# Decay rows of the gated delta rule through DRAM, one exponential for both masks, and both moved three to four blocks earlier

## The chip, the cores and the metric

One core of a Trainium2 chip runs the kernel. The metric is the device time of one execution in microseconds (us). The engines are TensorE (PE, matrix products and transposes), VectorE (DVE), ScalarE (ACT), GpSimd (POOL) and SyncE (SP, which issues most of the weight loads). ACT and POOL issue DMAs too, each on a queue of its own.

## What is computed

The kernel is one layer of a decoder trunk for 512 prompt tokens and 8 x 8 sample tokens (576 in all, five tiles of at most 128). The change lies in the gated delta rule:

```python
g = -exp(a_log) * softplus(a + dt_bias)      # per token and head, 4 heads
G = cumsum(g)                                # inside the chunk (here: a tile)
diff = G[:, None] - G[None, :]               # G falls, so diff <= 0 where i >= j
dec = where(i >= j, exp(diff), 0)
a_mat = where(i > j, kk * dec * beta[:, None], 0)
qk = (q @ k.T) * dec
eG = exp(G)                                  # scales q, and k in the right-hand side
```

The kernel needs, for each tile and head, the mask `A` (i > j), the mask `D2` (the same values transposed: j >= i along the row), and `E`, which is exp(G) of all tokens of the tile on all 128 partitions.

## The kernel before

Every engine walks the same list of steps, `schedule()`, and does what a step asks of it (the `elif k0 == ...` branches of `build()`, one block of branches for each engine). So the list sets the order of the work on each engine and of the DMAs that the engine issues, and semaphores tie the engines together: `mm_wait` waits for a step's products, `ev_wait` for its evacuation from PSUM.

The change lies in the part with the 12 causal convolutions. For each channel block m from 2 to 11 the list holds `cv` m (PE: 16 products that fill a pair of PSUM banks, line 818; ACT copies them to SBUF, line 1506), `cvt` m (DVE: the convolution, lines 2040 to 2055), `cvs` m-1 (ACT: SiLU of the block before, line 1605), and then `between[m]`, other work that is spread over the blocks:

- block 4, `rN`: PE sums the squares of the retention's output (line 972), ACT takes the root (line 1608), `nr`: DVE the reciprocal (line 2064). Block 5, `ns`: ACT stores the rows in DRAM (`n_rows`, line 1614). Block 6, `nl`: ACT loads four of them, each broadcast to 128 partitions (line 1625, 4 x 288 KB). Blocks 7 and 8, `nf`: DVE scales with them (line 2069).
- block 7, `gC`: PE makes the cumulative sums by token on the partitions (lines 1022 and 1024), DVE copies them to `gcum`.
- blocks 7 and 8, `gG` t: PE makes the same sums along the row, on all 128 partitions, as four products whose weight is one column of `gl` broadcast to 128 (line 1015); ACT copies the bank to `Gr[t]`. `gD` t: DVE makes `Gr - gcum`, clipped at 0 from below into `A` and from above into `D2`, head by head (lines 2096 and 2097).
- blocks 9 and 10, `gE` t: ACT takes three exponentials of 512 columns and two of four columns (lines 1654 to 1658); POOL multiplies `A` and `D2` by their 0/1 masks (lines 2838 and 2840). `gX`: DVE takes the last column of each `E`.
- blocks 9 and 10, `gs` t: PE transposes k (line 1031), ACT squares it with a sum (line 1632). On PE a `gs` waits for SiLU of channel block 7: `pe.wait_ge(sem("conv"), 8)`.
- block 11, `gr`: the reciprocal and root of the sums. After it `rg` 0 and the products `gK` and `gQ` (line 1039).

Steps of the kinds in `PAIR` take the two pairs of PSUM banks in turn, those in `SINGLE` the four single banks in turn; `bank_free` makes PE wait until the step that had the bank before was evacuated. So block m's convolution waits for the evacuation of the step two pairs before, and `gs` 4 for that of `gs` 0. An evacuation counts in one semaphore for all of ACT's, and ACT works in the list's order.

SyncE loads the weights in chunks of 2 MB into a ring of three; the chunk `dz` is issued when the last product of convolution block 7 is done (`mm_wait(sp, plan.chunk_last[n - RING])`). ACT changes its function table between SiLU, the exponential and the root; `link` makes ACT wait for the end of an instruction of its own.

Of the kernel before, what the change touches and what calls it, by code (L numbers as in the profile page):

```python
# [19 lines left out]
F32 = mybir.dt.float32  # L20
# [5 lines left out]
P = 128  # L26
# [4 lines left out]
NT = 5  # L31
# [39 lines left out]
def ntok(t):  # L71
    return P if t < 4 else NB * LS
# [96 lines left out]
def schedule():  # L169

    s = [("tk", k) for k in range(6)] + [("ss",), ("tk", 6), ("xr",)] + [("tmq", t) for t in range(NT)]
    for t in range(NT):
# [3 lines left out]
        if t: s += [("rS", t - 1)]  # L176
# [4 lines left out]
    between = {2: [("nq", "rN", m) for m in (0, 1)], 3: [("nq", "rN", m) for m in (2, 3)],  # L181
               4: [("rN",), ("nr", "rN")], 5: [("ns", "rN")], 6: [("nl", "rN")],
               7: nf("rN", (0, 1)) + [("gC",), ("gG", 0), ("gG", 1), ("gD", 0), ("gD", 1)],
               8: nf("rN", (2, 3)) + [("gG", t) for t in range(2, NT)] + [("gD", t) for t in range(2, NT)],
               9: [("gs", t) for t in range(3)] + [("gE", 0), ("gE", 1)],
               10: [("gs", 3), ("gs", 4)] + [("gE", t) for t in range(2, NT)] + [("gX",)], 11: [("gr",)]}
    for m in range(2, NCONV):
# [89 lines left out]
def first_phase(e):  # L277
# [14 lines left out]

ACT_EVAC = {"ss", "tmq", "tmv", "rTk", "rO", "sO", "rO4", "rOt", "sO4", "sOt", "cv", "rN", "oN", "rg", "gG", "gs", "ab", "x2a", "x2b", "rt", "gA", "lY", "gW", "gU", "dz",
            "wx", "ux", "pp"}
DVE_EVAC = {"xr", "abT", "rTq", "rS", "rU", "rUs", "gC", "gK", "gQ", "lX", "lT", "gV", "gk", "sD", "sDs", "sU", "sUs", "wo", "wy", "uy",
            "rtT", "rank", "cnt", "x2c"}
# [70 lines left out]
def build(nc, a, o):  # L367
# [5 lines left out]
    u_rows = nc.dram_tensor("u_rows", (TOK, D), F32, kind="Internal").ap()  # L373
    n_rows = nc.dram_tensor("n_rows", (2 * P, TOK), F32, kind="Internal").ap()
    y_slots = nc.dram_tensor("y_slots", (SLOTS, D), F32, kind="Internal").ap()

    with ExitStack() as ctx:
        def sb(name, shape, dt=F32):
            return ctx.enter_context(nc.sbuf_tensor(name, shape, dt))
# [23 lines left out]
        beta = sb("beta", [P, NT, H])  # L403
        gcum = sb("gcum", [P, NT, 8])
        gx = sb("gx", [P, NT, 8])
        sm = sb("sm", [P, 3, NT, H])
# [264 lines left out]
        def heads(s, n, w):  # L671
            return single[plan.buf[s]][0:n, 0:H * w].rearrange("p (h w) -> p h w", h=H)

        def tri(t):
            return C("tri") if t < 4 else C("tri_s", 64)
# [14 lines left out]
        def mm_wait(eng, s):  # L690

            eng.wait_ge(s_mm, plan.mm[s])
# [107 lines left out]
        def _(pe):  # L800
# [24 lines left out]
            for s in STEPS:  # L825
# [184 lines left out]
                elif k0 == "gG":  # L1010
                    t, n = s[1], ntok(s[1])
                    pe.wait_ge(sem("g_beta"), 1)
                    out = heads(s, P, n)
                    for h in range(H):
                        last = nc.tensor.matmul(out[:, h, :], gl[0:n, t, h:h + 1].broadcast_to([n, P]), tri(t),
                                                start=True, stop=True)
                    last.then_inc(s_mm, 1)
# [475 lines left out]
        def _(act):  # L1493
# [13 lines left out]
            for s in STEPS:  # L1507
# [138 lines left out]
                elif k0 == "gG":  # L1646
                    t, n = s[1], ntok(s[1])
                    mm_wait(act, s)
                    act.wait_ge(sem("ret_free"), 1)
                    copy(Gr[t], heads(s, P, n)).then_inc(ev(k0), 1)  # L1650
                elif k0 == "gE":
                    t, n = s[1], ntok(s[1])
                    act.wait_ge(sem("gdiff"), t + 1)
                    nc.scalar.activation(A[t], A[t], ACT.Exp, scale=-1.0).then_inc(sem("gexp"), 1)
                    nc.scalar.activation(D2[t], D2[t], ACT.Exp).then_inc(sem("gexp"), 1)
                    nc.scalar.activation(E[t], Gr[t], ACT.Exp).then_inc(sem("gexp"), 1)
# [269 lines left out]
        def _(dve):  # L1926
# [22 lines left out]
            for s in STEPS:  # L1949
# [132 lines left out]
                elif k0 == "gC":  # L2082
# [7 lines left out]
                    V.tensor_tensor(sm[0:64, 2, 4, :], gcum[0:64, 4, 4:8], gcum[0:64, 4, 0:4], ALU.subtract)  # L2090
                elif k0 == "gD":
                    t, n = s[1], ntok(s[1])
                    ev_wait(dve, ("gG", t))
                    for h in range(H):

                        V.tensor_scalar(A[t][:, h, :], Gr[t][0:n, h, :], gcum[0:n, t, h:h + 1], 0.0, ALU.subtract, ALU.max)
                        last = V.tensor_scalar(D2[t][:, h, :], Gr[t][0:n, h, :], gcum[0:n, t, h:h + 1], 0.0, ALU.subtract, ALU.min)
                    last.then_inc(sem("gdiff"), 1)
                elif k0 == "gX":
                    dve.wait_ge(sem("gexp"), 5 * NT)  # L2100
                    for t in range(NT):
# [666 lines left out]
        def _(pool):  # L2768
# [3 lines left out]
            for s in STEPS:  # L2772
# [59 lines left out]
                elif k0 == "gE":  # L2832
                    t, n = s[1], ntok(s[1])
                    if t == 0:
                        pool.wait_ge(sem("nfin"), 4)
                        G.memset(nwz, 0.0).then_inc(sem("zeroed"), 1)
                    pool.wait_ge(sem("gexp"), 5 * t + 1)
                    G.tensor_tensor(A[t], A[t], bh(C("low") if t < 4 else C("low_s", 64), n, n), ALU.mult).then_inc(sem("gmask"), 1)
                    pool.wait_ge(sem("gexp"), 5 * t + 2)
                    G.tensor_tensor(D2[t], D2[t], bh(tri(t), n, n), ALU.mult).then_inc(sem("gmask"), 1)  # L2840
# [200 lines left out]
```

## Time and profile before

| | us |
|---|---|
| median of 3 runs | 823.36 (823.05 to 825.56) |
| the profiled execution, its own time | 822.85 |
| its span, first to last instruction | 821.0 |
| PE busy | 802.8 (98%) |
| DVE busy | 405.6 (49%) |
| ACT busy | 214.8 (26%) |
| POOL busy | 152.6 (19%) |

The profile is one execution. The time of an execution holds some 2 us outside the span. In the rows a product of 32-bit floats counts as two records of PE (a transpose as one), L818 is line 818 of the kernel, and times are from the start of the span. "Idle before" names what released the engine. The engines PE and ACT start an instruction before the last one has left the pipeline, so starts tell more than durations.

### The profile page before, as it was taken

What the parts mean: (1) busy time and instruction counts of PE and PEld (TensorE: products, weight loads), DVE (VectorE), ACT (ScalarE), POOL (GpSimd) and SP (SyncE); (2) the same over time, 40 slices, a digit from 0 to 9 for tenths busy, and PEclk for the clock granted to TensorE, in tenths of its full rate; (3) what the DMA queues carried; (4) which work ended last, traced back from release to release, by engine and by line L of the source; (5) the groups of instructions that cost most, each with busy time, mean ns of one, the idle gap of its engine ahead of it and who ended that gap; (6) DMA issues with size and microseconds to landing.
All of it is one profiled execution on the core that took longest, in us unless ns stands there. A gap on an engine that the chain in (4) does not pass through costs nothing. (4 is left out here: it accounts for less than half of the span.)

```text
span 821.0 us, 12877 instructions
## 1 busy us (share of the span) xinstructions
PE 802.8 (98%) x5172; PEld 504.8 (61%) x5172; DVE 405.6 (49%) x886; ACT 214.8 (26%) x469; POOL 152.6 (19%) x182
## 2 busy tenths in 40 slices
PE   9999999999999999999999999999999999999995
PEld 4446777887889987777777776455433333334443
DVE  4223556684666522663853458826352101104976
ACT  3202152239324311131101110122121111125275
POOL 0324420004055223300220034000100001004100
PEclk9999999999999999999999999999999999999999
DMA  9521344503020200514241123134899999995211
GB/s 360 229 85 32 120 166 154 157 18 111 1 104 3 77 29 14 204 52 124 103 177 65 67 103 119 65 131 183 308 397 362 421 426 423 402 400 204 77 52 65
DMA packets 20977, 135.23 MB, mean 165 GB/s; under 512 B 2437, under 2 KB 3077, under 8 KB 13749
## 3 DMA queue, kind: packets, MB, share of 16 engines
q1 hardware_dynamic: 13328, 103.08, 32.1%
q0 software_dynamic: 4720, 23.83, 7.9%
q10 hardware_dynamic: 2868, 7.47, 3.0%
q8 instruction: 43, 0.70, 0.3%
q14 instruction: 18, 0.14, 0.0%
HBM read 118.94 MB, written 19.63 MB: 169 GB/s over the span
## 5 line engine op out<-in xcount | busy, mean ns | idle before, releaser
L818 PE MATMUL pair<-mem 128*128 128x288 f32 x640 | 158.9, 408 | 0.0
L818 PEld LDWEIGHTS pair<-mem 128*128 128x128 f32 x640 | 120.3, 190 | 35.6 <-ACT mem L1506 2.1
L986 PE MATMUL single<-mem 128*128 128x288 f32 x448 | 110.0, 407 | 0.2
L986 PEld LDWEIGHTS single<-mem 128*128 128x128 f32 x448 | 84.7, 190 | 25.7 <-issue 1.6
L1373 PE MATMUL single<-mem 128*32 128x512 f32 x768 | 85.1, 594 | 0.9 <-DVE mem L2539 0.9
L1506 ACT ACTIVATE mem<-pair 128x512 f32<-128x512 f32 (+5 forms) x83 | 36.5, 487 | 162.6 <-PE pair L818 63.1
L1506 ACT ACTIVATE mem<-single 128x256 f32<-128x256 f32 (+5 forms) x109 | 44.6, 419 | 126.9 <-PE single L1234 48.5
L2532 DVE SCALAR_TENSOR_TENSOR mem<-single,mem 128x256 f32<-128x256 f32 x12 | 5.8, 484 | 102.3 <-PE single L1373 91.4
L1373 PEld LDWEIGHTS single<-mem 128*32 128x32 f32 x768 | 23.6, 110 | 52.8 <-issue 51.7
L1225 PE MATMUL pair<-mem 128*128 128x512 f32 x112 | 51.0, 601 | 0.0
L1442 PE MATMUL pair<-mem 128*128 128x512 f32 x112 | 49.4, 595 | 0.3 <-DVE mem L2600 0.3
L2251 DVE TENSOR_TENSOR mem<-mem,single 128x288 f32<-128x288 f32 x40 | 18.1, 453 | 55.7 <-PE single L986 52.2
L1321 PE MATMUL pair<-mem 128*32 128x512 f32 x384 | 43.9, 595 | 0.0
L1442 PEld LDWEIGHTS pair<-mem 128*128 128x128 f32 x112 | 20.7, 190 | 25.2 <-issue 24.4
L1225 PEld LDWEIGHTS pair<-mem 128*128 128x128 f32 x112 | 20.3, 190 | 21.7 <-issue 21.4
L881 PE MATMUL pair<-mem 128*128 128x512 f32 (+1 forms) x96 | 32.1, 525 | 0.0
L2938 POOL DMA_INDIRECT mem<-u_rows,ids x12 | 11.4, 947 | 110.6 <-PE single L1306 100.8
L1007 PE MATMUL pair<-mem 128*128 128x288 f32 x112 | 28.4, 409 | 0.3 <-DVE mem L2303 0.2
L857 PE MATMUL pair<-mem 128*128 128x512 f32 x64 | 28.2, 595 | 0.4 <-DVE mem L1960 0.4
L2049 DVE SCALAR_TENSOR_TENSOR mem<-mem,vec 128x512 f32<-128x512 f32 x36 | 27.9, 774 | 1.3
L1007 PE MATMUL single<-mem 128*128 128x288 f32 x112 | 27.8, 406 | 0.0
L1007 PEld LDWEIGHTS pair<-mem 128*128 128x128 f32 x112 | 21.0, 190 | 7.0 <-DVE mem L2303 1.5
(431 smaller groups left out, 1118.1 us busy)
## 6 DMA issues: line engine op xcount, KB each, us to landing
mem<-in_w_gu SPq DMA_DIRECT2D x17, 2048.0 KB, 14.4
mem<-in_w_down SPq DMA_DIRECT2D x17, 1024.0 KB, 13.2
y_slots<-mem SPq DMA_DIRECT2D x9, 512.0 KB, 10.5
y_slots<-in_zeros POOLq DMA_DIRECT2D x8, 512.0 KB, 8.6
mem<-in_w_ga SPq DMA_DIRECT2D x2, 2048.0 KB, 7.7
mem<-in_w_gb SPq DMA_DIRECT2D x2, 2048.0 KB, 7.6
mem<-in_w_wo SPq DMA_DIRECT2D x2, 2048.0 KB, 7.7
mem<-in_w_pg SPq DMA_DIRECT2D x2, 2048.0 KB, 16.6
```

The lines of the kernel that those rows point to most:

```text
L818: last = nc.tensor.matmul(pb[:, hf, 0:HALF], w(k), rhs[:, k, hf * HALF:(hf + 1) * HALF], start=(k == 0), stop=(k == kk - 1))
L857: last = nc.tensor.matmul(q_bank[t][rows, cols], uT[:, k, t * P:t * P + ntok(t)], ring[0][:, 512 * k + cols.start:512 * k + cols.stop], st ...
L881: last = nc.tensor.matmul(pair[plan.buf[s]][rows, 0, cols], uT[:, k, t * P:t * P + ntok(t)], w[:, k, cols], start=(k == 0), stop=(k == KD ...
L986: last = nc.tensor.matmul(single[plan.buf[s]][:, 0:HALF], lhs[:, k, :], rhs[:, k, :], start=(k == 0 and j in (0, 1, 3, 4)), stop=(k == 3), ...
L1007: last = nc.tensor.matmul(fast_bank(s), lhs[:, k, :], rhs[:, k, :], start=(k == 0 and j in (0, 1, 3, 4)), stop=(k == 1), skip_group_check= ...
L1225: last = nc.tensor.matmul(sx_bank[j], rows[:, u, v, :], wgt[:, u, 512 * v:512 * v + 512], start=(i == 0 and j < 5), stop=(i == 3), skip_gr ...
L1321: last = nc.tensor.matmul(pair[p % 2][BS * g:BS * g + BS, n, :], hT[p % 2][:, k, BS * g:BS * g + BS], w_dn[e % 4][:, k, n * 512:(n + 1) * ...
L1373: last = nc.tensor.matmul(single[3][BS * g:BS * g + BS, :], xT[p % 2][:, k, BS * g:BS * g + BS], w_gu[e % 4][:, k, :], start=(k == 0), sto ...
L1442: last = nc.tensor.matmul(bank, rows(c), weights(c), start=(start and c == 0), stop=(c == 3), skip_group_check=True)
L1506: copy = lambda out, in_, scale=1.0: nc.scalar.activation(out, in_, ACT.Copy, scale=scale)
L2049: V.scalar_tensor_tensor(out=acc[m % 2][:, 0:LP], in0=cbuf[m % 2][:, j:j + LP], scalar=conv_w[:, m, j:j + 1], in1=acc[m % 2][:, 0:LP], op0 ...
L2251: V.tensor_tensor(to, plus, single[plan.buf[s]][:, 0:HALF], ALU.add).then_inc(ev(k0), 1)
```

## The change

`gC` and `gG` move to block 4, ahead of `rN`. `gG` is now one step: two products whose weights are `gl` itself (16 and 4 columns), so that the sums of all tiles and heads come out as rows on 20 partitions. DVE copies them to a new tile `grow`, ACT stores that in DRAM (`g_rows`, two DMAs), and in block 6 the new step `gL` loads five tiles of `Gr` from it, each broadcast to 128 partitions (4 x 256 KB, and 128 KB for tile 4, whose rows have 64 columns). `gD` goes. `gE` moves to blocks 7 and 8: ACT makes |Gr - gcum| with four `Abs` for each tile, then one exponential of its negative for both masks, and `E`; it waits until all five loads have landed. POOL writes `A` from `D2`, then masks `D2` in place. `gX` moves from block 10 to block 8. `gs` stays where it is, and k's squares are still made from transposes.

```diff
@@ schedule
-               4: [("rN",), ("nr", "rN")], 5: [("ns", "rN")], 6: [("nl", "rN")],
-               7: nf("rN", (0, 1)) + [("gC",), ("gG", 0), ("gG", 1), ("gD", 0), ("gD", 1)],
-               8: nf("rN", (2, 3)) + [("gG", t) for t in range(2, NT)] + [("gD", t) for t in range(2, NT)],
-               9: [("gs", t) for t in range(3)] + [("gE", 0), ("gE", 1)],
-               10: [("gs", 3), ("gs", 4)] + [("gE", t) for t in range(2, NT)] + [("gX",)], 11: [("gr",)]}
+               4: [("gC",), ("gG",), ("rN",), ("nr", "rN")], 5: [("ns", "rN")], 6: [("nl", "rN"), ("gL",)],
+               7: nf("rN", (0, 1)) + [("gE", 0), ("gE", 1)], 8: nf("rN", (2, 3)) + [("gE", t) for t in range(2, NT)] + [("gX",)],
+               9: [("gs", t) for t in range(3)], 10: [("gs", 3), ("gs", 4)], 11: [("gr",)]}
@@ TensorE, gG
-                    t, n = s[1], ntok(s[1])
                     pe.wait_ge(sem("g_beta"), 1)
-                    out = heads(s, P, n)
-                    for h in range(H):
-                        last = nc.tensor.matmul(out[:, h, :], gl[0:n, t, h:h + 1].broadcast_to([n, P]), tri(t),
-                                                start=True, stop=True)
+                    out = single[plan.buf[s]]
+                    nc.tensor.matmul(out[0:16, 0:P], gl[:, 0:4, :], tri(0), start=True, stop=True)
+                    last = nc.tensor.matmul(out[32:32 + H, 0:64], gl[0:64, 4, :], tri(4), start=True, stop=True)
                     last.then_inc(s_mm, 1)
@@ ScalarE, gG, gL and gE
-                    t, n = s[1], ntok(s[1])
-                    mm_wait(act, s)
+                    ev_wait(act, s)
+                    act.dma_start(g_rows[0:16, :], grow[0:16, :]).then_inc(sem("g_stored"), 16)
+                    act.dma_start(g_rows[16:20, 0:64], grow[32:36, 0:64]).then_inc(sem("g_stored"), 16)
+                elif k0 == "gL":
+                    act.wait_ge(sem("g_stored"), 32)
                     act.wait_ge(sem("ret_free"), 1)
-                    copy(Gr[t], heads(s, P, n)).then_inc(ev(k0), 1)
+                    for t in range(NT):
+                        n = ntok(t)
+                        act.dma_start(Gr[t], g_rows[4 * t:4 * t + 4, 0:n].unsqueeze(0).broadcast_to([P, H, n])).then_inc(sem("g_rows"), 16)
                 elif k0 == "gE":
                     t, n = s[1], ntok(s[1])
-                    act.wait_ge(sem("gdiff"), t + 1)
-                    nc.scalar.activation(A[t], A[t], ACT.Exp, scale=-1.0).then_inc(sem("gexp"), 1)
-                    nc.scalar.activation(D2[t], D2[t], ACT.Exp).then_inc(sem("gexp"), 1)
+                    ev_wait(act, ("gC",))
+                    act.wait_ge(sem("g_rows"), 16 * NT)
+                    for h in range(H):
+                        last = nc.scalar.activation(D2[t][:, h, :], Gr[t][0:n, h, :], ACT.Abs, bias=gcum[0:n, t, h:h + 1], scale=-1.0)
+                    link(last)
+                    nc.scalar.activation(D2[t], D2[t], ACT.Exp, scale=-1.0).then_inc(sem("gexp"), 1)
                     nc.scalar.activation(E[t], Gr[t], ACT.Exp).then_inc(sem("gexp"), 1)
@@ VectorE, gD goes, gG comes
-                elif k0 == "gD":
-                    t, n = s[1], ntok(s[1])
-                    ev_wait(dve, ("gG", t))
-                    for h in range(H):
-
-                        V.tensor_scalar(A[t][:, h, :], Gr[t][0:n, h, :], gcum[0:n, t, h:h + 1], 0.0, ALU.subtract, ALU.max)
-                        last = V.tensor_scalar(D2[t][:, h, :], Gr[t][0:n, h, :], gcum[0:n, t, h:h + 1], 0.0, ALU.subtract, ALU.min)
-                    last.then_inc(sem("gdiff"), 1)
+                elif k0 == "gG":
+                    mm_wait(dve, s)
+                    V.tensor_copy(grow[0:16, :], single[plan.buf[s]][0:16, 0:P])
+                    V.tensor_copy(grow[32:36, 0:64], single[plan.buf[s]][32:36, 0:64]).then_inc(ev(k0), 1)
@@ GpSimd, gE
-                    pool.wait_ge(sem("gexp"), 5 * t + 1)
-                    G.tensor_tensor(A[t], A[t], bh(C("low") if t < 4 else C("low_s", 64), n, n), ALU.mult).then_inc(sem("gmask"), 1)
-                    pool.wait_ge(sem("gexp"), 5 * t + 2)
+                    pool.wait_ge(sem("gexp"), 4 * t + 1)
+                    G.tensor_tensor(A[t], D2[t], bh(C("low") if t < 4 else C("low_s", 64), n, n), ALU.mult).then_inc(sem("gmask"), 1)
+                    pool.wait_ge(sem("gmask"), 2 * t + 1)
                     G.tensor_tensor(D2[t], D2[t], bh(tri(t), n, n), ALU.mult).then_inc(sem("gmask"), 1)
```

## Rows read from the trace of the kernel before

**Rows 1.** The page: span, and busy time by engine.
```profile
span 821.0 us, 12877 instructions
...
PE 802.8 (98%) x5172; PEld 504.8 (61%) x5172; DVE 405.6 (49%) x886; ACT 214.8 (26%) x469; POOL 152.6 (19%) x182
```

**Rows 2.** Windows: length, busy us by engine, PE clock, DMA share, GB/s.
```profile
85.00:205.00 120.00, 120.00 (x660) 92.17 (x659) 74.53 (x211) 52.38 (x140) 25.77 (x31) 1.00 0.34 114
```

**Rows 3.** PE in order of time: start, us, operation, count of records.
```profile
134.78 23.55 PE L818 MATMUL pair<-mem 128*128 128x288 f32 x96
158.17 0.52 PE L1022 MATMUL single<-gl,const 128*128 128x16 f32 x4
...
158.93 2.05 PE L1015 MATMUL single<-const,gl 128*128 128x128 f32 x16
160.82 7.93 PE L818 MATMUL pair<-mem 128*128 128x288 f32 x32
168.58 2.98 PE L1015 MATMUL single<-const,gl 128*128 128x128 f32 x24
171.49 8.03 PE L818 MATMUL pair<-mem 128*128 128x288 f32 x32
179.36 1.47 PE L1031 MATMUL single<-const,mem 128*128 128x128 f32 x12
...
188.43 1.04 PE L1031 MATMUL single<-const,mem 128*128 128x128 f32 x8
```

**Rows 4.** ACT's order of time, the last issues of `nl`.
```profile
151.52 0.94 ACTq L1625 DMA_DIRECT2D mem<-n_rows  x2
```

**Rows 5.** DVE's order of time, the reciprocal of block 4.
```profile
138.27 3.75 DVE L2064 RECIPROCAL mem<-mem 128x576 f32<-128x576 f32 x1
```

**Rows 6.** Line 1625, window 150 to 160: its DMAs.
```profile
L1625 ACTq DMA_DIRECT2D mem<-n_rows x4: 333/454/456, 150.7 to 152.0; - x4
...
DMA to landing us min/median/max: 3.7/5.7/6.8
```

**Rows 7.** Windows with `n_rows` loading, and with `dz` loading.
```profile
156.00:158.00 2.00, 2.00 (x10) 1.58 (x9) 0.00 (x0) 0.00 (x0) 0.00 (x0) 1.00 0.79 167
...
162.00:164.00 2.00, 2.00 (x10) 1.54 (x9) 2.00 (x4) 0.00 (x0) 0.00 (x0) 1.00 0.99 426
```

**Rows 8.** SyncE's order of time, the issue of `dz`.
```profile
158.36 0.33 SPq L715 DMA_DIRECT2D mem<-in_w_dz  x1
```

**Rows 9.** DMAs: SyncE's queue (q1), and ACT's third load.
```profile
q1 hardware_dynamic: 13328, 103.08, 32.1%
...
w_rt<-in_w_rt ACTq DMA_DIRECT2D x1, 128.0 KB, 4.8
```

**Rows 10.** ACT's order of time at the start of the kernel.
```profile
1.66 0.45 ACTq L1496 DMA_DIRECT2D w_rt<-in_w_rt  x1
...
6.26 0.68 ACT L1512 ACTIVATE mem<-mem 128x576 f32<-128x576 f32 x1 [1.35 <-DMA mem<-in_xT]
```

**Rows 11.** ACT's order of time in blocks 9 and 10.
```profile
184.01 1.28 ACT L1654 ACT_TABLE_LOAD   x1
185.31 0.63 ACT L1654 ACTIVATE mem<-mem 128x512 f32<-128x512 f32 x1
185.84 0.61 ACT L1655 ACTIVATE mem<-mem 128x512 f32<-128x512 f32 x1
...
187.07 0.61 ACT L1654 ACTIVATE mem<-mem 128x512 f32<-128x512 f32 x1
...
191.46 0.26 ACT L1632 ACTIVATE mem<-single 128x128 f32<-128x128 f32 x1
191.62 0.19 ACT L1632 ACTIVATION_READ_ACCUMULATOR mem<-single 128x1 f32 x1
```

**Rows 12.** ACT's order of time, copies with and without a pointer.
```profile
62.60 0.69 ACT L1569 ACTIVATE mem<-pair,rcol 128x512 f32<-128x512 f32 x1 [8.73 <-PE single L956]
63.19 0.59 ACT L1506 ACTIVATE mem<-pair 128x512 f32<-128x512 f32 x1
```

More of the change, by code:

```diff
@@ L290 @@
             "wo": lambda s: 13 + s[2]}
-ACT_EVAC = {"ss", "tmq", "tmv", "rTk", "rO", "sO", "rO4", "rOt", "sO4", "sOt", "cv", "rN", "oN", "rg", "gG", "gs", "ab", "x2a", "x2b", "rt", "gA", "lY", "gW", "gU", "dz",
+ACT_EVAC = {"ss", "tmq", "tmv", "rTk", "rO", "sO", "rO4", "rOt", "sO4", "sOt", "cv", "rN", "oN", "rg", "gs", "ab", "x2a", "x2b", "rt", "gA", "lY", "gW", "gU", "dz",
             "wx", "ux", "pp"}
-DVE_EVAC = {"xr", "abT", "rTq", "rS", "rU", "rUs", "gC", "gK", "gQ", "lX", "lT", "gV", "gk", "sD", "sDs", "sU", "sUs", "wo", "wy", "uy",
+DVE_EVAC = {"xr", "abT", "rTq", "rS", "rU", "rUs", "gC", "gG", "gK", "gQ", "lX", "lT", "gV", "gk", "sD", "sDs", "sU", "sUs", "wo", "wy", "uy",
             "rtT", "rank", "cnt", "x2c"}
@@ L374, in build @@
     n_rows = nc.dram_tensor("n_rows", (2 * P, TOK), F32, kind="Internal").ap()
+    g_rows = nc.dram_tensor("g_rows", (NT * H, P), F32, kind="Internal").ap()
     y_slots = nc.dram_tensor("y_slots", (SLOTS, D), F32, kind="Internal").ap()
@@ L404, in build @@
         gcum = sb("gcum", [P, NT, 8])
+        grow = sb("grow", [P, P])
         gx = sb("gx", [P, NT, 8])
@@ L2090, in _ @@
                     V.tensor_tensor(sm[0:64, 2, 4, :], gcum[0:64, 4, 4:8], gcum[0:64, 4, 0:4], ALU.subtract)
-                elif k0 == "gD":
-                    t, n = s[1], ntok(s[1])
-                    ev_wait(dve, ("gG", t))
-                    for h in range(H):
-                        V.tensor_scalar(A[t][:, h, :], Gr[t][0:n, h, :], gcum[0:n, t, h:h + 1], 0.0, ALU.subtract, ALU.max)
-                        last = V.tensor_scalar(D2[t][:, h, :], Gr[t][0:n, h, :], gcum[0:n, t, h:h + 1], 0.0, ALU.subtract, ALU.min)
-                    last.then_inc(sem("gdiff"), 1)
+                elif k0 == "gG":
+                    mm_wait(dve, s)
+                    V.tensor_copy(grow[0:16, :], single[plan.buf[s]][0:16, 0:P])
+                    V.tensor_copy(grow[32:36, 0:64], single[plan.buf[s]][32:36, 0:64]).then_inc(ev(k0), 1)
                 elif k0 == "gX":
-                    dve.wait_ge(sem("gexp"), 5 * NT)
+                    dve.wait_ge(sem("gexp"), 4 * NT)
                     for t in range(NT):
```

## Prediction

> **What bounds the kernel now.** I read the page first: TensorE (PE) is busy for 98% of the span, VectorE (DVE) for half of it, ScalarE (ACT) for a quarter [rows 1]. The reader is to see that only PE's time, or a wait of PE, can move the end. The busy times by stage say the same of the place of the change: between 85 and 205 us PE is busy for all of the 120 us, at full granted clock [rows 2]. So an instruction removed from PE there shortens the kernel by its whole cost, and other work costs nothing until it makes PE wait. PE's own order of time gives the beat [rows 3]: the 96 records of convolution blocks 5 to 7 (32 a block) take 23.4 us, 7.8 a block. Lastly I read ACT's order of time and its DMAs, since the change hands ACT the new work [rows 4 to 12].
>
> **What goes from PE.** The 20 products `gG` (40 records, 16 and 24) fill 158.93 to 160.82 and 168.58 to 171.49, thus 1.89 + 2.91 = 4.80 us [rows 3]. Two products take their place in block 4: one of 128 columns, one of 64, with few weight columns. A `gG` product took 0.24 us; `gC`'s first two took 0.52 with far fewer columns [rows 3]. Between 0.2 and 0.5, I take 0.4. `gC` moves and costs the same. PE gains 4.4 us in all; the bounds are 4.3 and 4.6.
>
> **DVE and POOL.** `gD`'s 40 instructions go, from cover (no PE wait is there), so they bring nothing. The masks on POOL stay ten instructions; the second of each tile now waits for the first, and they are done before `gK` is evacuated, tens of us later. They may meet DVE's convolution of block 9; each convolution has a block of cover. Nothing.
>
> **Block 4.** ACT now waits there for `gG`'s evacuation before it does `rN`'s root, and the root, the table load and all of ACT behind it wait too. DVE does it after convolution 4, so from 138.27, where the reciprocal `nr` began [rows 5]: some 0.9 us of small copies, two DMA issues at 0.47 [rows 4], a table load of 1.28 and the root of 0.74 put the root's end near 142.1. PE needs that bank at block 6, at 134.78 + 1.2 + 7.8 = 143.8 (the 1.2 is what `gC` and `gG` add to block 4). It is covered by 1.7 us. `nr` then ends near 145.8, and its row is stored 2 us later, before the loads of block 6. Nothing, if the issues stay under 1.2 us each.
>
> **The five loads of `gL`: when the rows are there.** They stand on ACT's queue behind the four loads of `n_rows`. These were issued until 152.5 and landed 3.7 to 6.8 us after issue [rows 4, 6], as if one after another, so the last near 158.6; the block now starts 1.2 later, so 159.8. The DMA windows show that the 4 x 288 KB moved at some 170 GB/s with the engines 79% busy [rows 7], which makes 6.7 us of them, and by the landings, from 152 on, 6.2: a broadcast of rows is slow. `gL` is 4 x 256 KB of the same kind (1024/1152 of 6.2: 5.5) and a fifth of 128 KB, whose rows of 64 columns are 512 pieces of 256 B. By bytes it is 0.7 us, by pieces (n_rows had as many) 6.2; I take 2. Alone they would be there at 159.8 + 5.5 + 2 = 167.3 (166.0 to 171.5).
>
> They are not alone. SyncE issues the 2 MB of `dz` when block 7 ends on PE, at 158.4 before [rows 8] and 159.5 now. At 426 GB/s [rows 7] that is 4.9 us of all engines. At the start of the kernel, where both queues are full, the third DMA of ACT's queue landed at 1.66 + 4.8 = 6.5 us, and ACT's second piece of xT, the third DMA of SyncE's, at 6.26 [rows 9, 10]: the queues advance turn by turn. SyncE's packets are large (7.7 KB) and few, `gL`'s small and many [rows 9], so all of `dz` gets in before `gL` ends. That makes 172.2; without any delay 167.3. I take 171, and 166 to 173 as the bounds.
>
> The Trainium skill ("DMA: Bandwidth & Descriptors", Queues, rings and completion order) says that each engine goes round between the queues packet by packet, draining a whole packet of several descriptors; by it `dz` is in front of the last of `gL` too, and the sum would be that of 172. The trace agrees in the start's two landings, as far as they go.
>
> **ACT from there.** `gE` of tile 0 waits for all five rows; behind it on ACT stand `gE` 1, the evacuation of block 8, `silu` 7, `gE` 2 to 4, the evacuation of block 9, `silu` 8 and `gs` 0. PE waits for two of them: `gs` 0 on PE needs `silu` 7, and `gs` 4 on PE takes the bank that ACT frees with `gs` 0 (the fourth single bank before it). Costs:
> - A tile's three exponentials and two small ones took 187.07 - 185.31 = 1.76 [rows 11]; its exponentials start 0.53 apart, so one less leaves 1.24. Four `Abs` of 128 columns with a pointer bias are not in the trace. The nearest are the 128-column instructions of `gs`, 0.27 long, the next operation 0.16 later [rows 11], and 512 columns with a pointer scale, 0.69 against about 0.60 without [rows 12]. So 0.16 to 0.29 apart, and the link waits out the last. I take 1.2 for four (0.7 to 1.3): 2.45 a tile. Tile 4 (half the columns): about 1.8. Five tiles: 11.6.
> - Two loads of the exponential table and two back, 1.28 each [rows 11]: 5.1. Two `silu`: 1.3. Two evacuations: 1.5. `gs` 0: 1.0, and 0.1 of signals.
> Sum 20.6 us from the landing (18.5 to 21.5). The Trainium skill ("ScalarE: Activation LUTs", What ACT_TABLE_LOAD costs) adds 1.38 us of drain to each load; here the exponential starts 1.30 after the load began [rows 11], so the trace disagrees. By the page the chain would be 5.5 longer.
>
> **The sum.** PE wants `gs` 4 at 188.43 + 0.44 - 4.4 = 184.5 [rows 3]. Landing 171 + 20.6 = 191.6, so PE waits 7.1 us: about 5.0 at `gs` 0 (171 + 9.0 for `gE` 0, 1, table loads, evacuation and `silu` 7 = 180.0, against 179.36 - 4.4 = 175.0), the rest at `gs` 4. What stands later (block 11's evacuation, the key norms, `gK`) has a block's cover again. Net: -4.4 + 7.1 = **+2.7 us**. The profiled execution took 822.85 (span 821.0 and 1.85 around it), so 825.6 for it; its time is 0.5 under the median of 823.36, so the median comes to **826.1**. Break-even is a landing at 168.3; the full gain needs 163.9.
>
> **Rivals.**
> 1. The rows are there at about 167, because `dz` and the broadcasts overlap (the engines are not full during `n_rows`). Wait 3.1, net -1.3: 822.1. Against: the two landings at the start.
> 2. (Other side.) ACT's chain has the cover. The mechanism is one: the rows land by 163.9 on ACT's queue (the broadcast of short rows runs at the rate of `dz`, 1.15 MB in 2.7 us, from 159.8 or earlier). Then nothing waits, 4.4 is gained: 819.0. For: PE had not one wait from 85 to 205, and ACT was busy 52 of those 120 us [rows 2]. Against: `n_rows` at half that rate. It is faster than the measurement can tell up to a landing of 165.8.
> 3. `Abs` needs a table that has no exponential. Then each tile loads twice: 2.57 x 5 = 12.8 more, 839. Against: copies and squares run between `silu`s with no load. The Trainium skill ("ScalarE: Activation LUTs", Table sets) lists abs in every set, which the runs will show.
> 4. The fifth load costs its 6.2 us by pieces, or a wait of 5 us on PE brings more behind it (a lower granted clock, which no row here shows after such a wait). Net +7: 830.
>
> **How the numbers follow.** The chance of the forecast is 0.50 (its own range 824 to 829: landing 169 to 172.5, chain 20 to 21.5), of rival 1 0.20, rival 2 0.18, rival 3 0.02, rival 4 0.10. What a measurement can tell from no change is 0.3%, 2.5 us: faster is under 820.9, slower over 825.8. Rival 2 and a little of rival 1 make faster: 0.20. Most of rival 1 and the forecast with a landing below 170.7 make the same: 0.32. The rest, 0.48, is slower. The range takes in a landing of 168 with the shortest `Abs` (net -2.4) up to one of 173 with the long chain (+5.6): 820.9 to 829.0.
>
> **What would show it.** In the changed profile: PE's blocks 5 to 8 in one piece and about 1.2 us late; block 9 right behind block 8, 3.2 early in total; DMAs of `g_rows` landing 15 us or more after issue, the last near 171; an ACT wait of about 10 us before the first `Abs`, released by that DMA; PE idle some 5 us before `gs` 0 and 2 before `gs` 4, released by ACT; no PE wait at blocks 5 and 6; `gK` starting 2.7 later than 204.82. The prediction is wrong if the rows land before 166, if `Abs` runs in 0.16 us, or if PE's `gs` has no wait.

## The result, and the profile after

The changed kernel took **826.96 us** (median of 11 runs, 823.96 to 831.54), the kernel before beside it 823.24 (11 runs, 822.82 to 825.94): ratio 1.0040, 95% interval 1.0021 to 1.0059. It is slower by 3.7 us, against a forecast of 826.1. Note the range: 7.6 us for the changed kernel, 3.1 for the other. The changed kernel was measured a second time, beside later experiments: 825.43, ratio 1.0021.

The page of the changed kernel, to be read against [rows 1]: PE works 2.3 us less, yet the span is 4.1 longer.

```profile
span 825.1 us, 12781 instructions
...
PE 800.5 (97%) x5136; PEld 501.5 (61%) x5136; DVE 400.7 (49%) x848; ACT 216.1 (26%) x479; POOL 152.8 (19%) x182
```

PE in order of time, over the stretch of [rows 3]:

```profile
134.45 0.39 PE L1013 MATMUL single<-const,gl 128*16 128x128 f32 x2
134.78 0.27 PE L1014 MATMUL single<-const,gl 64*4 64x64 f32 x2
134.98 1.18 PE L972 MATMUL pair<-mem,const 128*32 128x288 f32 x16
136.09 39.07 PE L818 MATMUL pair<-mem 128*128 128x288 f32 x160
179.21 2.08 PE L1029 MATMUL single<-const,mem 128*128 128x128 f32 x12 [4.06 <-ACT mem L1603]
181.09 9.06 PE L818 MATMUL pair<-mem 128*128 128x288 f32 x32
189.99 0.60 PE L1029 MATMUL single<-const,mem 128*128 128x128 f32 x4
191.05 0.63 PE L1029 MATMUL single<-const,mem 128*64 128x128 f32 x4 [0.46 <-ACT mem L1630]
191.51 15.69 PE L818 MATMUL pair<-mem 128*128 128x288 f32 x64
207.03 5.19 PE L1037 MATMUL single<-mem 128*128 128x128 f32 x45
```

The two products that replace the 20 take 0.53 us (134.45 to 134.98). Blocks 5 to 9 now run in one piece of 160 records. Then PE waits 4.06 us in front of `gs` 0, for silu 7 (SiLU of channel block 7, L1603). Block 10, 7.93 us long before, takes 9.06. The windows say why (window, its length, PE's busy time and records, granted clock, DMA share, GB/s):

```profile
178.00:180.00 2.00, 0.79 (x7) 0.99 0.00 0
180.00:182.00 2.00, 2.00 (x9) 0.50 0.00 0
182.00:184.00 2.00, 2.00 (x7) 0.65 0.00 0
184.00:186.00 2.00, 2.00 (x10) 1.00 0.00 0
```

After the wait PE ran for some 3.4 us at the lower of its two levels (1.2 GHz); before the wait it had been busy without a gap. The last four records of `gs` wait 0.46 more. `gK` starts at 207.03, 2.21 later than before.

ACT in order of time, from the issue of the loads to the first masks:

```profile
153.87 5.73 ACTq L1655 DMA_DIRECT2D mem<-g_rows  x5
159.78 0.41 ACT L1504 ACTIVATE mem<-pair 128x288 f32<-128x288 f32 x1 [6.52 <-PE pair L818]
...
169.95 1.28 ACT L1661 ACTIVATE mem<-mem,gcum 128x128 f32<-128x128 f32 x4 [8.83 <-DMA mem<-g_rows]
171.24 1.28 ACT L1663 ACT_TABLE_LOAD   x1
172.54 0.63 ACT L1663 ACTIVATE mem<-mem 128x512 f32<-128x512 f32 x1
...
173.78 1.26 ACT L1661 ACTIVATE mem<-mem,gcum 128x128 f32<-128x128 f32 x4
175.07 0.63 ACT L1663 ACTIVATE mem<-mem 128x512 f32<-128x512 f32 x1
...
178.38 0.68 ACT L1603 ACTIVATE mem<-mem 128x576 f32<-128x576 f32 x1
...
189.28 0.68 ACT L1603 ACTIVATE mem<-mem 128x576 f32<-128x576 f32 x1
189.87 0.26 ACT L1630 ACTIVATE mem<-single 128x128 f32<-128x128 f32 x1
```

ACT stood for 8.83 us until the rows were there, at 169.9. From then on it has no gap up to `gs` 0, which frees the bank that PE takes at 191.05. Line 1655, the five loads:

```profile
L1655 ACTq DMA_DIRECT2D mem<-g_rows x5: 387/1269/1527, 153.9 to 158.5; - x5
...
DMA to landing us min/median/max: 7.4/8.3/11.3
```

### The profile page after: what moved, and what is told of

Read it like the earlier page. It is cut to its first block and busy times, and to the rows that moved or that the text cites. A ratio compares the mean times of both kernels' runs of the same rounds, so it can differ in the third digit from the quotient of the medians.

```text
span 825.1 us, 12781 instructions
## 1 busy us (share of the span) xinstructions
PE 800.5 (97%) x5136; PEld 501.5 (61%) x5136; DVE 400.7 (49%) x848; ACT 216.1 (26%) x479; POOL 152.8 (19%) x182
## 5 line engine op out<-in xcount | busy, mean ns | idle before, releaser
L818 PE MATMUL pair<-mem 128*128 128x288 f32 x640 | 159.6, 410 | 0.0
L1504 ACT ACTIVATE mem<-single 128x256 f32<-128x256 f32 (+6 forms) x104 | 41.9, 413 | 126.9 <-PE single L1232 48.5
L1319 PE MATMUL pair<-mem 128*32 128x512 f32 x384 | 43.9, 595 | 0.0
```

Source lines behind the costliest of these rows:

```text
L818: last = nc.tensor.matmul(pb[:, hf, 0:HALF], w(k), rhs[:, k, hf * HALF:(hf + 1) * HALF], start=(k == 0), stop=(k == kk - 1))
L1319: last = nc.tensor.matmul(pair[p % 2][BS * g:BS * g + BS, n, :], hT[p % 2][:, k, BS * g:BS * g + BS], w_dn[e % 4][:, k, n * 512:(n + 1) * ...
L1504: copy = lambda out, in_, scale=1.0: nc.scalar.activation(out, in_, ACT.Copy, scale=scale)
```

## The experiments

The reading to be tested: the loss is the landing of the rows plus ACT's chain behind it, all else is covered. The first four runs take the change apart. Each time is the median, with the lowest and highest in brackets, and each ratio is to the kernel before measured beside it.

**Rows a block earlier.** In block 6's list the copies stand; here in block 5's:

```
-  5: [("ns", "rN")], 6: [("nl", "rN"), ("gL",)],
+  5: [("ns", "rN"), ("gL",)], 6: [("nl", "rN")],
```

> The changed kernel with the copies of the decay rows (gL: stores by ACT, loads back by ACT's queue) in block 5 instead of block 6, three blocks ahead of the exponentials; nothing else differs. Theory (the chain behind the landing is on the path only because the rows land at 169.9): the rows land near 155 to 160, the first decay mask is made 10 us sooner, PE never waits for ACT in front of gs, its clock stays at 1.00 there, and the time is about 819 us, 0.5% under the kernel before. Rival A (the ACT work of block 7 itself, table loads and the pointer biases, is too long for the slot wherever the rows are): ACT is late again, a wait of 2 us or more in front of the gs products stays, and the time is 823 or more. Rival B (stores and loads in block 5 delay the column norms' scratch round trip or the evacuation of convolution 6): a new wait of PE near 100 to 140, time 821 or more.

Measured: 820.22 (819.63 to 822.07, 7 runs; before 823.16), ratio 0.9963 (0.9950 to 0.9976). The five issues took 2.34 us in place of 5.73, the loads landed 3.9 to 4.9 us after issue, ACT began the first `Abs` at 160.97 behind silu 6 without a wait, and PE ran through:

```profile
175.07 1.47 PE L1029 MATMUL single<-const,mem 128*128 128x128 f32 x12
176.38 7.93 PE L818 MATMUL pair<-mem 128*128 128x288 f32 x32
184.14 1.04 PE L1029 MATMUL single<-const,mem 128*128 128x128 f32 x8
185.01 15.69 PE L818 MATMUL pair<-mem 128*128 128x288 f32 x64
200.54 8.38 PE L1037 MATMUL single<-mem 128*128 128x128 f32 x80
```

`gK` starts 4.28 earlier than before: that is the saving on PE in full, so the landing's theory holds and both rivals fall. But the end came only 3.2 earlier (span 817.8), not 4.3, and the time is 1.2 above the 819 expected. The missing 1.1 is the subject of the last group.

**`dz` later.** SyncE issues `dz` only when PE has done convolution 9, so that it no longer moves beside the rows.

```
+                if name == "dz":
+                    mm_wait(sp, ("cv", 9))
```

> The changed kernel with one more wait: SP loads dz only when PE has done convolution 9, so that the big load is no longer beside the rows' load back. Theory (some of the landing time is the shared engines): the rows land 3 to 4 us sooner, near 166, PE waits under 1 us and its clock does not drop, time about 821 to 822 us. Rival (the rows' load takes what it takes, because of its small pieces and broadcast reads): landing stays at 169 to 170, time 826 to 827. If dz itself comes too late, a wait near its first use shows it.

Measured: 822.77 (821.35 to 823.73, 10 runs), ratio 0.9983 (0.9973 to 0.9994); profiled run: rows at 165.7, PE waits 1.3 us at `gs` 4 and nowhere else, clock at 1.00. The range shrank to 2.4 us. So `dz` beside the loads costs 4.2 us of median against the first measurement of the changed kernel, 2.7 against the second. PE's wait was a little over the 1 us expected.

**Exponentials where they were.** `gE` and `gX` in blocks 9 and 10, copies of the rows in block 6.

> The changed kernel with the exponentials and masks (gE, gX) back in blocks 9 and 10, where the kernel before has them; the copies of the rows stay in block 6. Theory (the loss comes from ACT waiting in block 7 on rows that are not there, with silu 7 queued behind): no such wait, PE runs through, the gain of the products left out comes out in full, 819 us. Rival (the move is harmless and the form costs: Abs, pointer bias, DMA beside the convolutions): a wait moves to block 9 or later and the time is 823 to 827.

Measured: 824.54 (822.96 to 826.40, 12 runs), ratio 1.0011 (1.0001 to 1.0020). There was no wait at `gs`, but one at `gK`, as the rival had it.

**The single exponential alone.** The kernel before without `gD`: ACT makes the four `Abs` and one exponential of each tile in blocks 9 and 10. ScalarE's part of the edit (DVE's `gD` goes, and POOL reads `D2`, as in the change):

```
-                    act.wait_ge(sem("gdiff"), t + 1)
-                    nc.scalar.activation(A[t], A[t], ACT.Exp, scale=-1.0).then_inc(sem("gexp"), 1)
-                    nc.scalar.activation(D2[t], D2[t], ACT.Exp).then_inc(sem("gexp"), 1)
+                    ev_wait(act, ("gC",))
+                    ev_wait(act, ("gG", t))
+                    for h in range(H):
+                        last = nc.scalar.activation(D2[t][:, h, :], Gr[t][0:n, h, :], ACT.Abs, bias=gcum[0:n, t, h:h + 1], scale=-1.0)
+                    link(last)
+                    nc.scalar.activation(D2[t], D2[t], ACT.Exp, scale=-1.0).then_inc(sem("gexp"), 1)
```

> The kernel before with one part alone: one exponential of minus the absolute difference serves both masks; the rows are still made by products on PE and the work stays in its old blocks. Theory (ACT is off the path there): no change, 823.3 us, within 0.3%. Rival (Abs sits in another table set than Exp): ten more table loads in the trace and 823 to 830 us.

Measured: **827.88** (825.32 to 828.99, 6 runs), ratio 1.0047 (1.0032 to 1.0061). The table-set rival fell too: no load stands between `Abs` and the exponential of a second tile. So the theories of both runs fell, in the same place. PE of the single exponential alone, in order of time:

```profile
206.76 3.73 PE L1039 MATMUL single<-mem 128*128 128x128 f32 x32
212.77 6.54 PE L1039 MATMUL single<-mem 128*128 128x128 f32 x48 [2.27 <-DVE mem L2120]
```

and DVE in the same stretch:

```profile
205.31 0.32 DVE L2099 COPY glast<-mem 128x4 f32<-128x4 f32 x1 [7.75 <-ACT gx L1661]
...
207.77 0.75 DVE L2052 SCALAR_TENSOR_TENSOR mem<-mem,vec 128x512 f32<-128x512 f32 x1
...
211.59 1.13 DVE L2120 SCALAR_TENSOR_TENSOR mem<-single,kr,mem 128x128 f32<-128x128 f32 x4
```

A tile now takes ACT 2.54 us in place of 1.76 [rows 11], for four short instructions cost more than one long one saves. Over five tiles that is 3.7 us: DVE's `gX`, which waits 7.75 us for ACT, begins at 205.31 against 199.65, of which 1.94 are this execution's later start. The taps of a convolution stand behind `gX` on DVE, and behind them the first evacuation of `gK`, for which PE waits 2.27 us. Then it runs at half clock again. With the exponentials back in blocks 9 and 10, where the wait is the same 2.27, the windows (PE alone, in the order given above) show

```profile
204.00:206.00 2.00, 0.28 (x3) 1.00 0.00 0
206.00:208.00 2.00, 1.45 (x7) 0.57 0.00 0
208.00:210.00 2.00, 2.00 (x12) 0.57 0.00 0
```

2.27 of wait and 1.75 of half clock are 4.0 us: from `gK`'s start to the next block it is 12.34 us (200.55 to 212.89), 8.32 before. So ACT's work in blocks 9 and 10 was not free. In the kernel before, DVE's first evacuation of `gK` ended near 207.4 and PE wanted the bank 3.73 after its start, at 208.55: it was 1.2 us ahead.

**Smaller pieces.** Tile 4's rows in a tensor of their own (`g_tail`), so that its load has 128 pieces of 1 KB in place of 512 of 256 B.

> The changed kernel with tile 4's rows in a contiguous tensor of their own, so that its load back has 128 pieces of 1 KB in place of 512 of 256 B; block 6 as before. Theory of the prediction (tile 4's small pieces cost 2 us of the landing, 0.7 to 6.2): the first load lands 1 to 2 us sooner than 169.9, the wait of PE in front of gs 0 falls from 4.1 to 2 or 3 us, time 824 to 825.5. Rival (the five loads share one 5 us stretch with dz, and bytes set it): landing within 0.5 us of 169.9, time 826.5 to 827.5.

Measured: 823.55 (821.11 to 826.89, 10 runs), ratio 1.0009 (0.9990 to 1.0027).

**Busy wait.** Spare products on PE in front of `gs` 0:

```
+                    if t == 0:
+                        for i in range(14):
+                            nc.tensor.matmul(single[plan.buf[s]][:, 0:P], C("ones"), C("tri"), start=True, stop=True)
```

> The changed kernel with 14 spare products of 128 columns (about 3.4 us) written to gs 0's bank before PE waits for silu 7; they are overwritten and change no result. PE is thus busy for most of the 4.1 us that it waits in the changed kernel. Theory (the wait also costs the clock, 1.7 us after it): the granted clock stays at 1.00 from 180 to 184 and the time is 825 us or a little more, 1.2 to 1.9 under the changed kernel's in the same job. Rival (the clock falls anyway or its loss is not 1.7): 826.5 to 828.

Measured: 825.00 (821.52 to 829.82, 10 runs), ratio 1.0031 (1.0008 to 1.0053).

These two are inconclusive, and taught something else. In the profiled run with spare products the loads were the changed kernel's to the letter, but ACT began at 164.97, so there was no wait that the products could have filled. The median lies 2 us under the first measurement of the changed kernel and 0.4 under the second, below. What the clock costs was thus not measured, but the first profile of the changed kernel argues that a full clock would have brought nothing there. PE reaches the last four records of `gs` at 190.59 and waits until 191.05, when ACT's chain gives the bank. Had block 10 run at full clock, PE would have waited there for as much longer. By this reading my price of 1.7 us for the clock was wrong: half clock took the place of waiting.

**Both in block 5, and 72 waits.** First the tail's tensor with the copies in block 5.

> The copies of the rows in block 5 and tile 4's rows in a tensor of their own, both. Theory (in block 5 the landing has some 5 us to spare, so small pieces cost nothing there): equal to the version with block 5 alone, 820.2 us within 0.5, and PE waits nowhere for ACT in front of gs. Rival (small pieces disturb other transfers too): 0.5 us or more under it.

Measured: 820.34 (819.60 to 820.90, 6 runs), ratio 0.9965 (0.9953 to 0.9978), as its theory had it: in block 5 the small pieces cost nothing. Then the same with waits in PE's stream, in front of the products of each step k of convolutions 2 to 10:

```
+                    if s[0] == "cv" and 2 <= s[1] <= 10:
+                        pe.wait_ge(sem("rtmp_ones"), 1)
```

> The same as the kernel with block 5 and the tail's own tensor, with 72 waits on a semaphore that has long been there added to PE's stream, one in front of each k step of convolutions 2 to 10: they cost PE nothing while its products run, and put PE's later instructions 72 places further on, about where they stand in the kernel before. In the changed kernel and in the three variants without the 20 products, PE stands for 1.43 us at one and the same product of L1060, near 245, with nothing that the trace shows it waiting for; in the kernel before and in the one that keeps the products, it does not. Theory (this pause depends on the place of the instructions in PE's stream): it is gone or at another place, and the time is about 1.4 us under the kernel without the waits, near 818.8. Rival (it comes from other engines or from DMA at that time): the pause of 1.43 stays at that product and the time is the same, 820.2.

Measured: 820.75 (819.49 to 821.64, 10 runs), ratio 0.9971 (0.9962 to 0.9981). It said nothing on its question: its page counts 12781 instructions, as without the waits, so they made PE's stream no longer. It is a second measurement of the kernel above.

**The changed kernel again, and a semaphore for each load.** The first has no edit. In the second, where the wait for all five loads stood before tile 0, each tile waits for its own (the loads' side of the edit is left out here):

```
-                    act.wait_ge(sem("g_rows"), 16 * NT)
+                    act.wait_ge(sem(("g_rows", "ld_vec", "ld_const", "ld_small", "ld_head")[t]), (16, 32, 32, 64, 32)[t])
```

Each load adds 16 to a semaphore of its own; four of them served loads of the kernel's start and stand at a known count.

> The changed kernel once more, nothing altered, beside the two others. In the profiled runs so far the last of the five loads of the rows landed at 169.9 (changed kernel), and near 165 in the two variants with the same copies in block 6 and dz at the same time. Theory (the last load lands either ahead of dz's transfer or behind it, by chance of the execution, and that is where the changed kernel's wide range of times comes from): median 825 to 828, range over 4 us; if this profiled run lands at 165, it has a span of 820 to 822 and no wait in front of gs 0. Rival (those variants landed early for what they change): landing at 169.5 to 170.5 again, span 824 to 826.

> The changed kernel with a semaphore of its own for each of the five loads of the rows, so that tile 0's absolute differences wait for tile 0's rows alone and not for all five; copies in block 6, dz and all else as in the changed kernel. Theory (only the last load is late; the first lands near 161.5, and ACT's work of 2.5 us a tile keeps behind the landings): ACT starts tile 0 near 161.5, PE waits nowhere in front of gs, span 817.5 to 819, time 820.0 to 820.8, and the range is as narrow as in the kernel with the copies in block 5. Rival (the loads land together, or a later tile's load holds ACT up): ACT waits 2 us or more in a later tile, time 822 to 827.

Measured: the changed kernel again 825.43 (822.45 to 827.68, 10 runs), ratio 1.0021 (1.0006 to 1.0035). Its profiled run, in PE's order of time:

```profile
177.76 1.50 PE L1029 MATMUL single<-const,mem 128*128 128x128 f32 x12
179.10 7.93 PE L818 MATMUL pair<-mem 128*128 128x288 f32 x32
186.86 0.60 PE L1029 MATMUL single<-const,mem 128*128 128x128 f32 x4
189.60 0.63 PE L1029 MATMUL single<-const,mem 128*64 128x128 f32 x4 [2.14 <-ACT mem L1630]
```

No wait at `gs` 0, full clock, 2.14 us at `gs` 4. (The span, 823.6, misses the 820 to 822 expected since this execution had lost 2.5 us by block 4, in its first 30 us; such losses of up to 2.5 us came in executions of several kernels, such as 1.9 in the one with the single exponential alone; their cause was not looked for.) ACT began the masks 31.0 us after PE began `rN` (168.49 against 137.47), in the first profile 35.0 (169.95 against 134.98), and in the runs with the tail's tensor, the spare products and `dz` later 30.8, 29.9 and 29.8. The longest landing was 8.4 us in these, 11.3 in the first, and 11.9 with the exponentials in blocks 9 and 10. The DMA view of the stretch of the issues, first profile and then second, tells which load it is:

```profile
mem<-g_rows ACTq DMA_DIRECT2D x4, 256.0 KB, 8.2
mem<-g_rows ACTq DMA_DIRECT2D x1, 128.0 KB, 11.3
...
mem<-g_rows ACTq DMA_DIRECT2D x4, 256.0 KB, 8.0
mem<-g_rows ACTq DMA_DIRECT2D x1, 128.0 KB, 7.5
```

The load of tile 4 alone is late. Over the seven profiled runs with the copies in block 6 the other four have a median of 7.9 to 8.6 us from issue to landing; tile 4's takes 11.3 and 11.9 in two of them and 6.4 to 7.5 in five (7.1 of these with its pieces of 1 KB, 6.4 without `dz`). So with `dz` beside the loads, tile 4's comes some 4 to 5 us later in some executions than in others. That, and the losses of the first 30 us, are what the profiles show of the changed kernel's wide range; the highest time, 831.54, is 2 us more than the two together give (826.89 and 2.5), and was not profiled.

With a semaphore for each load: **820.57** (819.72 to 822.30, 7 runs), ratio 0.9968 (0.9956 to 0.9980), as its theory said. ACT starts tile 0 at 163.26, and PE has no wait at `gs`, although the loads landed as late as 9.1 us after issue (tile 4's, in this execution, 6.9):

```profile
163.26 1.28 ACT L1662 ACTIVATE mem<-mem,gcum 128x128 f32<-128x128 f32 x4 [1.71 <-DMA mem<-g_rows]
```

Thus not the rows as such were late: tile 0 waited for tile 4's. That the range is as narrow as with the copies in block 5 suggests that a late load of tile 4 no longer matters; no profile caught one.

**The rows alone.** Last, the other half of the change: sums in block 4 and DRAM copies in block 5, the differences on DVE, the two exponentials and the scaling in their old blocks.

> The kernel before with the rows alone changed: sums of 16 and 4 rows made in block 4, stored and loaded back through DRAM in block 5; the differences on DVE (blocks 7 and 8), the two exponentials and the scaling (blocks 9 and 10) as in the kernel before. Theory (the products left out give 4.2 us, a pause of 1.4 us comes at L1060, and the single exponential with its 20 small absolute differences is what cost 4.7 us where it was tried alone in the old place): 820 to 821 us, 2 to 3 under the kernel before. PE now comes 4.3 us sooner to gK, whose first bank DVE had free 1.25 us before PE wanted it; if ACT's work of blocks 9 and 10 does not move forward with PE, PE waits there for DVE, up to 3 us, and the clock may fall after it: 821 to 825. Rival (the cost of the single exponential in the old place came from the earlier PE or from the place, not from the form): a wait of 2.3 us at gK and half clock here too, 824 to 825.

Measured: 820.33 (819.88 to 824.01, 5 runs), ratio 0.9965 (0.9951 to 0.9979). No wait at `gK`: PE's 80 records took 8.38 us. ACT's and DVE's work there moved forward with PE (DVE's first evacuation ended near 204.9, and PE wanted the bank at 206.0). The whole gain is in the rows; the single exponential adds none, and costs 4.7 us in blocks 9 and 10.

**The pause at L1060.** In all ten profiled runs that leave the products out and add nothing to PE's stream, PE stood for 1.2 to 1.7 us before one and the same record, the 175th of the inverse's leaves (64 columns each), with nothing that the trace shows it waiting for. Here in the kernel with the copies in block 5:

```profile
239.72 1.10 PE L1060 MATMUL single<-mem 64*64 64x64 f32 x29
242.25 1.65 PE L1060 MATMUL single<-mem 64*64 64x64 f32 x41 [1.43 <-issue]
```

To move the place of PE's later instructions, 18 spare products of one column were put in front of `gs` 0 in that kernel:

> The kernel with the copies in block 5, and 18 spare products of one column in front of gs 0 (written to its bank and overwritten), which put back about as many instructions in PE's stream as the products left out had (72 of the 72 that the page counts fewer on PE). The 72 added waits of the run before were not in the program that ran: its page counts 12781 instructions, as without them, so that run said nothing. In the run with 14 spare products (55 instructions more on its page) the pause of L1060 came 27 records earlier. Theory (the pause is tied to a place in PE's instruction stream, and falls on short products of L1060 only because 18 products are gone): no pause of over 0.5 us at L1060, and the time is 820.2 plus what the 36 short records cost (1 to 2.5 us) less 1.4, so 820 to 821.5. Rival (the pause belongs to the work of that moment): 1.2 to 1.4 us at the same product, time 821 to 822.7.

Measured: 828.36 (827.25 to 829.63, 4 runs), ratio 1.0068 (1.0053 to 1.0082), far outside what I expected: 36 records of one column took 4.37 us, 0.12 each (the 1 to 2.5 us expected are 0.03 to 0.07), and from 180.8, while they still ran, the clock was at half for 3.4 us, though PE's records show no gap. But its 71 more instructions moved the pause 35 records forward, out of L1060's products:

```profile
245.11 2.21 PE L1084 MATMUL single<-mem 64*64 64x64 f32 x66
248.94 0.39 PE L1084 MATMUL single<-mem 64*64 64x64 f32 x4 [1.62 <-issue]
```

In the run with 14 spare products, 55 more instructions moved it 27 records forward. A record is two instructions (weights and product), so 70 and 54: the pause sits at a fixed place in PE's stream of instructions. The theory that PE has no such pause at all once its stream is as long as in the kernel before fell. What is loaded at such a place can be seen in the DMA view of single stretches: the queue named instruction moves packets of 16 KB. With the copies in block 5, from 240 to 242:

```profile
q1 hardware_dynamic: 46, 0.57, 68.6%
q8 instruction: 1, 0.02, 3.0%
```

The next such packet comes from 242 to 244, then one from 246 to 248. The 2 MB of `in_w_ga` (q1, issued at 234.82) move just ahead of and beside the first of them, and fill the engines from 238 to 240. In the kernel before such a packet came from 236 to 238, before that load (issued at 239.10), and the next from 244 to 246. I take it that PE's next instructions were late because their packet was behind the weights' packets: argued from the trace, not tried (the way would be to move `in_w_ga`).

## Why the prediction was right

By its steps:

- **PE's saving**: forecast 4.4, measured 4.28 (`gK` in the kernel with the copies in block 5); the two new products took 0.53, not 0.4.
- **DVE and POOL, nothing**: right for this schedule, with the exponentials in blocks 7 and 8. That it was nothing is owed to the move: in blocks 9 and 10 ACT's extra 0.78 us a tile came through DVE to PE as 4 us. I had looked for PE's waits there and found none, but not for how far DVE was ahead.
- **Block 4**: the root ended at 142.44 (forecast 142.1), PE had its bank in time. The proviso, issues under 1.2 us each, held for the two stores (0.35 and 0.57). The sum had no term for the issues of the five loads of block 6, 1.27 us the median one. They held ACT until 159.6, and it evacuated convolution 7 at 159.78, just in time. So the loads landed 7.4 to 11.3 after issue, not 15 or more; the rest of the delay was in the issuing.
- **Landing**: forecast 171 (166 to 173), 169.9 in this profile, about 4 to 5 us sooner in others: two outcomes, and the forecast value was the late one. That the profile of the result was a late one is luck. `dz` is the cause that I gave, and taking it away brought 2.7 to 4.2 us. Without it I had the landing at 167.3. Counted from PE's `rN` as in the first profile, it came at 164.8, which is 2.5 sooner. The late outcome is then 5.1 later, about the 4.9 of a whole `dz`; the others are 0.1 to 1.2 later. So `dz` in front of the last of `gL`, as I had it, is what some executions show, for tile 4's load alone. The forecast of 171 comes near since the loads themselves were priced 2.5 too high, and `dz` (3.7 of its 4.9) 1.4 too low for this outcome. The Trainium skill ("DMA: Bandwidth & Descriptors", Queues, rings and completion order), by which an engine goes round the queues packet by packet, allows it; why that load is late in one execution and not in the next stays open. Its small pieces (2 us in the sum) cost nothing where it was not late (6.4 to 7.5 us, and 7.1 in pieces of 1 KB); whether they have a part in the late outcome was not told apart.
- **ACT's chain**: 20.6 forecast, 169.95 to 191.05 is 21.1. Tiles 2.54 (2.45), no table load between the `Abs` and the exponential of tile 1 (173.78, 175.07), as the Trainium skill's page on activations ("ScalarE: Activation LUTs", Table sets) has it; the exponential again began 1.30 after its load began (171.24, 172.54), so the 1.38 us of drain that the same page adds do not show.
- **The wait**: 7.1 us forecast. Compared with the kernel with the copies in block 5, the records behind `gs` 4 start 6.5 later (191.51, 185.01): 4.06 and 0.46 of wait, 1.1 more for block 10 and 0.6 for the first twelve records of `gs` at half clock (0.3 is left over). Right as a sum; the clock took the place of most of the wait at `gs` 4.
- **The sum**: +2.7 forecast at `gK`, +2.2 there. The profiled execution then lost 1.0 by the pause in L1060 (net: by L1319, the last block of PE's work ahead of the tail, it is 729.44 against 726.25), and 0.8 in the tail: from there to the last group of products but one (L1484, L1486 before) it took 76.5 us in place of 75.7. The chain that ended last goes there through DMAs, where that of the kernel before goes over PE's products:

```profile
729.44 3.57 PE pair L1319 x32
739.83 5.92 DMA y_slots<-mem
747.82 5.86 DMA mem<-y_slots,posu
```

  Neither was in the sum. So +4.1 in the span, +3.7 in the median: the nearness to 826.1 is partly luck, an overestimate of 0.5 and an omission of 1.8 that went opposite ways. The second measurement, 825.43, lies as near on the other side.
- **Break-even**: full gain was put at a landing of 163.9. The run with the tail's tensor waits 2.15 us with a start at 165.72, thus 163.6.
- **Rivals**: 1 (rows near 167) is near what the executions without the late load show, with rows at 164.9 to 166.0 and 822.02 and 823.01 us in two of them. Rival 4's fall of the clock came, by the reading above at no cost of its own; 3 fell. 2, the gain in full at `gK`, needed the copies a block earlier or a semaphore for each load, and came to 820.2 and not 819.0.

The version to keep is any of three, 820.2 to 820.6, 2.4 to 2.9 us under the kernel before, which the runs do not tell apart: copies in block 5, a semaphore for each load, or the rows alone with the old exponentials.

## What to carry to other kernels

When several loads feed work that takes them one by one, give each its own semaphore: the one wait for all five cost this kernel its gain, and made its time depend on how the last load fared against an unrelated 2 MB transfer. Before calling an engine's work covered, find the engine that stands between it and the bottleneck and read how far ahead that one is: here 1.2 us, and 0.78 us a tile used it up. A change made of two parts is best measured in two: one part here gave 2.6 us, the other nothing at best and a loss of 4.7 in its old place.

## What the hardware showed unexpectedly

- ACT's DMA issues, 0.39 us for the first, took a median of 1.27 and up to 1.53 when four broadcast loads were ahead of them; in block 5 the same five took 0.38 to 0.47 each.
- PE's granted clock fell to 1.2 GHz for 3.4 us after a wait of 4.06, and after one of 2.27 at `gK`, but not after 2.14 or 2.15 at `gs` 4. It fell too during 18 products of one column (36 records), when PE's records show no gap.
- The same load of 128 KB, issued at the same place of the program just before a 2 MB load on another queue, landed 6.5 to 7.5 us after issue in some executions and 11.3 to 11.9 in others, while the four of 256 KB ahead of it kept to a median of about 8.
- Products of one column in fp32 took 0.12 us a record (the last 0.7 us of the 4.37 at half clock).
- PE can stand for 1.2 to 2.0 us at a fixed place of its instruction stream. That a packet of instructions was late there, behind a large weight load, is argued and was not tried.
